# Moving a per-head normalisation and its bias tile from VectorE to GpSimd, in the differential attention of a two-block transformer kernel

## What is computed

```python
s  = einsum(q, k) * 64**-0.5 + slope[head] * (k_pos - q_pos)     # for both maps, masked to k <= q
a  = softmax(s[map 0]) - lam * softmax(s[map 1])
o  = a @ v                                                       # 512 x 128 for one head
o  = rms_norm(o, out_g) * (1 - lam_init)                         # over the 128 channels of the head
y  = o * silu(az)
```

## Time and profile before

| | us |
|---|---|
| median of 3 runs (2393.18 to 2393.83) | 2393.45 |
| the profiled execution | 2402.3 |
| its span | 2400.5 |
| TensorE busy | 2286.0 (95%) |
| VectorE busy | 1370.9 (57%) |
| ScalarE busy | 1004.8 (42%) |
| GpSimd busy | 262.2 (11%) |
| granted TensorE clock, mean | 0.972 |

### The profile page before, as it was taken

The page is one execution under the profiler, slowest core; times in us unless marked ns, Lnnn a source line. Parts: engine busy times, 40 slices in busy tenths (PEclk is TensorE's granted clock), DMA queues, the critical chain, the costliest instruction groups (busy, mean ns, idle before and its releaser), DMA issues. The chain is left out here.

```text
span 2400.5 us, 30388 instructions
## 1 busy us (share of the span) xinstructions
PE 2286.0 (95%) x11223; PEld 1849.9 (77%) x11223; DVE 1370.9 (57%) x2905; ACT 1004.8 (42%) x1896; POOL 262.2 (11%) x350
## 2 busy tenths in 40 slices
PE   5899989899999999999889999999999989999999
PEld 4777767688777787778778888888878657888887
DVE  6956676756746454554563455445455595545543
ACT  5545645433454545453323333233434583322322
POOL 3641000016101011100000000000011240000000
PEclk9999999899999999999877999999999999999999
DMA  7354112134332222225474232232322102233222
GB/s 207 119 163 140 54 53 88 36 106 141 106 102 71 84 92 84 75 75 184 134 200 109 76 104 86 92 105 88 105 88 88 53 2 71 88 105 106 80 88 96
DMA packets 192800, 236.73 MB, mean 99 GB/s; under 512 B 38827, under 2 KB 120194, under 8 KB 192654
## 3 DMA queue, kind: packets, MB, share of 16 engines
q1 hardware_dynamic: 170910, 211.93, 27.8%
q10 hardware_dynamic: 21744, 22.84, 3.0%
HBM read 215.84 MB, written 23.09 MB: 100 GB/s over the span
## 5 line engine op out<-in xcount | busy, mean ns | idle before, releaser
L2125 PE MATMUL G<-w_hi,u_hi 128*128 128x512 f32 x1536 | 624.3, 406 | 10.8 <-issue 5.6
L1666 DVE SCALAR_TENSOR_TENSOR w_lo<-raw,par,w_hi 128x512 fp32r<-128x512 f32 x496 | 368.1, 782 | 433.9 <-ACT w_hi L1134 431.0
L2127 PE MATMUL G<-w_hi,u_lo 128*128 128x512 f32 x1536 | 602.6, 392 | 0.0
L2126 PE MATMUL G<-w_lo,u_hi 128*128 128x512 f32 x1536 | 601.9, 392 | 0.0
L1134 ACT ACTIVATE w_hi<-raw,par 128x512 fp32r<-128x512 f32 x496 | 317.5, 715 | 378.4 <-PE G L2127 365.0
L2125 PE MATMUL G<-u_hi,w_hi 128*128 128x512 f32 (+1 forms) x1168 | 462.1, 396 | 11.8 <-DVE u_lo L1732 11.8
L2126 PE MATMUL G<-u_lo,w_hi 128*128 128x512 f32 (+1 forms) x1168 | 450.1, 385 | 0.0
L2127 PE MATMUL G<-u_hi,w_lo 128*128 128x512 f32 (+1 forms) x1168 | 450.0, 385 | 0.0
L2125 PEld LDWEIGHTS G<-w_hi,u_hi 128*128 128x128 f32 x1536 | 290.5, 189 | 78.7 <-issue 13.3
L2127 PEld LDWEIGHTS G<-w_hi,u_lo 128*128 128x128 f32 x1536 | 290.4, 189 | 63.2
L2126 PEld LDWEIGHTS G<-w_lo,u_hi 128*128 128x128 f32 x1536 | 290.9, 189 | 60.0 <-issue 1.9
(11 more groups left out here) (304 smaller groups left out, 2389.0 us busy)
## 6 DMA issues: line engine op xcount, KB each, us to landing
raw<-in_ffn_w_up SPq DMA_DIRECT2D x88, 512.0 KB, 4.6
raw<-in_e_w_in SPq DMA_DIRECT2D x56, 512.0 KB, 4.7
raw<-in_o_w_in SPq DMA_DIRECT2D x56, 512.0 KB, 4.5
raw<-in_ffn_w_down SPq DMA_DIRECT2D x40, 512.0 KB, 4.4
raw<-in_e_w_out SPq DMA_DIRECT2D x16, 512.0 KB, 4.6
raw<-in_o_w_out SPq DMA_DIRECT2D x16, 512.0 KB, 4.2
raw<-in_a_w_glu SPq DMA_DIRECT2D x16, 512.0 KB, 4.4
raw<-in_w_kv SPq DMA_DIRECT2D x16, 512.0 KB, 4.3
```

What stands on the lines that cost most here:

```text
L1666: V.scalar_tensor_tensor(w_lo[:, n % HL, k], raw[:, n % RAW, k], gain(name, k0 + k), w_hi[:, n % HL, k].bitcast(F32), ALU.mult, ALU.subtract)\
L2125: pe.matmul(out, lh, rh, start=start, stop=False)
L2126: pe.matmul(out, lh, rl, start=False, stop=False)
L2127: return pe.matmul(out, ll, rh, start=False, stop=stop)
```

## The change

The normalisation of a head's output and the bias of a head go from VectorE to GpSimd. ScalarE sums the squares itself, in four instructions with an accumulator where there was one. GpSimd then issues 17 linked instructions on 128x4 values (VectorE's form had 12, with one shift and three fused ones; here are a conversion through float and plain products) and the 128x512 product. The bias of an odd head lies in `big[:, 18]`, that of an even one in `junk[:, 1]`, and each has a semaphore `bias_ready`. VectorE's product to `y` goes from the end of the BACK slot to its beginning. GpSimd's work for heads 0 and 1 stands at the group's first unit, for heads 2 and 3 five units later, between the squares of two query and key chunks.

```diff
@@ Pool
+            def pool_bias(s, hd):
+                before, t = (s, 4 * hd - 5) if hd > 1 else (s.scored, len(s.scored.steps) - 1)
+                pool.wait_ge(*at_("score", before.i, t))
+                if hd == 1 and before.akind == "X":
+                    pool.wait_ge(*at_("y", before.i, before.heads - 1))
+                pool.tensor_scalar(head_bias(hd), bias_tile[:, :], 2.0 ** -(s.y0 + hd + 1), None, ALU.mult)\
+                    .then_inc(*by("bias_ready", s.i, hd))
+
+            def pool_head_norm(s, hd):
+                tt, ts = pool.tensor_tensor, pool.tensor_scalar
+                on = junk[:, 0, :].rearrange("p (a b) -> p a b", b=P)
+                pool.wait_ge(*at_("o_squared", s.i, hd))
+                do(ts(oss, oss, 1.0 / P, EPS, ALU.mult, ALU.add))
+                do(pool.tensor_copy(oln, oss.bitcast(I32)))
+                do(ts(oln, oln, -0.5, float(0x5f3759df), ALU.mult, ALU.add))
+                do(pool.tensor_copy(orstd.bitcast(I32), oln))
+                do(ts(oss, oss, -0.5, None, ALU.mult))
+                for _ in range(3):
+                    do(tt(oln, orstd, orstd, ALU.mult))
+                    do(tt(oln, oln, oss, ALU.mult))
+                    do(ts(oln, oln, 1.5, None, ALU.add))
+                    do(tt(orstd, orstd, oln, ALU.mult))
+                pool.wait_ge(*at_("o_copied", s.i, hd))
+                tt(on, o_copy.rearrange("p (a b) -> p a b", b=P), orstd.unsqueeze(2).to_broadcast([P, TT, P]), ALU.mult)\
+                    .then_inc(*by("on_ready", s.i, hd))
...
+                for s in a_mix:
+                    if s.n == n:
+                        for hd in range(3):
+                            pool_bias(s, hd)
+                        pool_head_norm(s, 0)
+                        pool_bias(s, 3)
+                        pool_head_norm(s, 1)
+                    if s.n + 5 == n:
+                        pool_head_norm(s, 2)
+                        pool_head_norm(s, 3)
@@ Activation
-                    nc.scalar.activation(junk[:, 0, :], X[:, s.aux["pv", hd] % 4, :], ACT.Square)\
-                        .then_inc(*by("o_squared", s.i, hd))
+                    for i in range(TT):
+                        c = slice(P * i, P * i + P)
+                        ins = nc.scalar.activation(junk[:, 0, c], X[:, s.aux["pv", hd] % 4, c], ACT.Square,
+                                                   accum_out=oss[:, i:i + 1])
+                    ins.then_inc(*by("o_squared", s.i, hd))
@@ DVE, dve_slot
+                if is_last(s, t - BACK) and s.akind == "A":
+                    hd = s.steps[t - BACK][0]
+                    y = big[:, s.y0 + hd, :]
+                    a = s.aux["ot", hd]
+                    dve.wait_ge(*at_("gate", s.gate, hd))
+                    dve.wait_ge(*at_("aux_ready", a))
+                    V.scalar_tensor_tensor(y, X[:, a % 4, :], gain("aout"), y, ALU.mult, ALU.mult)\
+                        .then_inc(*by("y", s.i, hd))
                 if t < T:
...
                     if s.akind == "A" and i == 0:
-                        link("dve", dve, V.tensor_scalar(junk[:, 1, :], bias_tile[:, :], 2.0 ** -(head + 1), None,
-                                                         ALU.mult))
+                        dve.wait_ge(*at_("bias_ready", s.i, hd))
...
-                    if s.akind == "A":
-                        on = junk[:, 0, :].rearrange("p (a b) -> p a b", b=P)
-                        dve.wait_ge(*at_("o_squared", s.i, hd))
-                        link("dve", dve, V.tensor_reduce(oss, on, AX_X, ALU.add))
-                        inverse_rms(orstd, oss, P, oln)
-                        dve.wait_ge(*at_("o_copied", s.i, hd))
-                        V.tensor_tensor(on, o_copy.rearrange("p (a b) -> p a b", b=P),
-                                        orstd.unsqueeze(2).to_broadcast([P, TT, P]), ALU.mult)\
-                            .then_inc(*by("on_ready", s.i, hd))
...
-                if is_last(s, t - BACK) and s.akind == "A":
-                    hd = s.steps[t - BACK][0]
-                    y = big[:, s.y0 + hd, :]
-                    a = s.aux["ot", hd]
-                    dve.wait_ge(*at_("gate", s.gate, hd))
-                    dve.wait_ge(*at_("aux_ready", a))
-                    V.scalar_tensor_tensor(y, X[:, a % 4, :], gain("aout"), y, ALU.mult, ALU.mult)\
-                        .then_inc(*by("y", s.i, hd))
```

More of the change, by code:

```diff
@@ L420, in attention @@
             s.n = state["n"]
+            if kind == "A":
+                a_mix.append(s)
+                for hd in range(heads):
+                    mark("bias_ready", s.i, hd)
             s.steps = [(hd, TT - 1 - i if kind == "C" else i) for hd in range(heads) for i in range(TT)]
@@ L528, in plan_ffn @@
             plan_down(22).first_y = first_y
+        a_mix = []
         def plan_even():
@@ L548, in plan_even @@
                              ("v", "N", dict(dst=8))], hosts)
+                scored = before
                 before, at = attention("A", 4, 4 * g, len(plan)), 7
-                if g == 0:
-                    a_mix = before
+                before.scored = scored
                 plan_chunks([("silu", "T", dict(dst=4 * g))], [(before, -1)])
@@ L555, in plan_even @@
             state["e_down"] = plan_down(16)
-            state["e_down"].first_y = ("y", a_mix.i, 3)
+            state["e_down"].first_y = ("y", a_mix[0].i, 3)
         c_mix = []
@@ L807, in scores, with head_bias @@
             return (att[:, 16 + m, :], att[:, 18 + m, :], third)[t % 3]
+        def head_bias(hd):
+            return big[:, 18, :] if hd % 2 else junk[:, 1, :]
         def sb_keep(t):
@@ L1811, in dve_slot @@
                             if s.akind == "A":
-                                b = junk[:, 1, 384 - P * i:512]
+                                b = head_bias(hd)[:, 384 - P * i:512]
                             else:
@@ L1837, in dve_slot @@
                             .then_inc(*by("p_ready", s.i, t - 1))
-                if is_last(s, t - VALUE):
+                if is_last(s, t - VALUE) and s.akind != "A":
                     hd = s.steps[t - VALUE][0]
                     y = big[:, s.y0 + hd, :]
-                    if s.akind == "A":
-                        on = junk[:, 0, :].rearrange("p (a b) -> p a b", b=P)
-                        dve.wait_ge(*at_("o_squared", s.i, hd))
-                        link("dve", dve, V.tensor_reduce(oss, on, AX_X, ALU.add))
-                        inverse_rms(orstd, oss, P, oln)
-                        dve.wait_ge(*at_("o_copied", s.i, hd))
-                        V.tensor_tensor(on, o_copy.rearrange("p (a b) -> p a b", b=P),
-                                        orstd.unsqueeze(2).to_broadcast([P, TT, P]), ALU.mult)\
-                            .then_inc(*by("on_ready", s.i, hd))
-                    else:
-                        a = s.aux["pv", hd]
-                        dve.wait_ge(*at_("gate", s.gate, hd))
-                        dve.wait_ge(*at_("aux_ready", a))
-                        V.tensor_tensor(y, X[:, a % 4, :], y, ALU.mult).then_inc(*by("y", s.i, hd))
-                if is_last(s, t - BACK) and s.akind == "A":
-                    hd = s.steps[t - BACK][0]
-                    y = big[:, s.y0 + hd, :]
-                    a = s.aux["ot", hd]
+                    a = s.aux["pv", hd]
                     dve.wait_ge(*at_("gate", s.gate, hd))
                     dve.wait_ge(*at_("aux_ready", a))
-                    V.scalar_tensor_tensor(y, X[:, a % 4, :], gain("aout"), y, ALU.mult, ALU.mult)\
-                        .then_inc(*by("y", s.i, hd))
+                    V.tensor_tensor(y, X[:, a % 4, :], y, ALU.mult).then_inc(*by("y", s.i, hd))
             def dve_prep(s, t):
```

## The result

The changed kernel takes 2402.79 us (median of 6 runs, 2399.14 to 2407.49), the kernel before 2394.91 us in the runs beside it: ratio 1.0031, 95% interval 1.0018 to 1.0045, which is 4 to 11 us more. One of the six executions of the kernel before took 3770.46 us and is not in the ratio; the median of the other five is 2393.83 us. The sign is as forecast, the size is not: 27 us were forecast. The profiled execution is 2403.86 us with a span of 2402.1 us. The profiled execution of before lay above its own median, so the two spans can't be subtracted from each other; the stage can be compared by its events.

A forecast was written before the change was run, and what follows sets the result against it. TensorE, busy 95%, was taken as the bound, so only its waits count: +34 new waits, -18.7 old waits, +20 clock lost, -8.7 clock regained is +27 us, 2420 us, stated as 2419; range 2384 to 2452.

The forecast's parts named there:

- The bound and the waits removed: TensorE's waits in the differential attention: 18.7 us in all, of which 9.3 us for y and 5.8 us for scores go.
- The new wait: TensorE in the BACK slot waits for GpSimd's normalised output: chain 10.4 us against 6.1 us, 4.3 us per head, 34 us.
- Squares to the first small instruction: ScalarE's four squares with accumulators, 1.6 us, and 0.1 us to hand over: 1.7 us per head.
- Small instructions: 17 linked ones on GpSimd at 0.27 us, 4.6 us per head, plus 2.8 us of disturbance by VectorE.
- Product and hand-over: GpSimd's 128x512 product, 1.06 us, 1.1 us with its hand-over, per head.
- The clock: Each of eight 4.3 us waits lowers TensorE's clock: 20 us lost, against 8.7 us gained from waits removed.
- Of my rivals the first: Same GpSimd wait, but the clock falls no more than now: +16 us, 2409 us; chance 0.15.
- rival 2: GpSimd's chain runs undisturbed, 7.6 us; TensorE waits 1.5 us per head; net -12 us, 2381 us; chance 0.17.
- Rivals 3 and 4: 3: chain disturbed all through, +70 us, 2463 us, chance 0.10; 4: waits only change names, 2393 us, chance 0.06.
- GpSimd's other work: Squares per chunk shift by some us, hidden; three early biases, about 0.6 us each, are made slots ahead.

The follow-up runs named there:

- e1: Kernel before with VectorE's y of a finished head put first in its slot, nothing moved to GpSimd; ratio to before 0.9962.
- e4: Changed kernel with the BACK slot one later (7 for 6), so TensorE asks for the normalised output later; ratio to before 0.9907.
- e8: Changed kernel with nine more linked 128x4 instructions in GpSimd's chain of each head; ratio to before 1.0150.
- e12: Changed kernel with VectorE filling w_lo with zeros in units 18 to 31 instead of computing it; ratio to before 0.9988.
- e3: Changed kernel with the normalisation back on VectorE and one square instruction on ScalarE; biases stay on GpSimd, y first; ratio to before 0.9957.
- e5: Kernel before with only the BACK slot one later; ratio to before 0.9978.

## Why the prediction was wrong, point by point

**The bound and the waits removed: right.** The 18.7 us of waits were the right account. e1 shows that y first takes 8 of the 9.3 us of y waits; with the normalisation off VectorE the score waits are gone in the changed kernel.

**The new wait: right mechanism, a failed size, 34 us forecast, 23.5 us measured.** TensorE's slack from the squares' start came out at 6.0 us (forecast 6.1 us). The chain was 8.9 us where I had 10.4 us. By terms:
- Squares to the first small instruction: 1.2 us for 1.7 us. A 128x128 square with its accumulator repeats every 0.25 us; I had taken the exponential's 0.40 us.
- Small instructions: 6.6 us on average for 4.6 + 2.8 us. Undisturbed ones repeat every 0.28 us (0.27 us forecast), 4.8 us for 17; the disturbance is 1.8 us, not 2.8 us. I counted all of VectorE's time with these instructions in 8 us after the squares as delay, but the small instructions run for 6.6 us only, and one that is held lasts as long as VectorE's beside it, with its own 0.28 us inside that time. In head 0 VectorE's weights and w_lo pieces run for 3.3 us beside the chain and delay it by 2.2 us.
- Product and hand-over: 1.1 us, as forecast; the further 0.2 us for hand-overs was counted twice.

So 1.5 us per head too much, 11 to 12 us for eight.

One reading was wrong beside it: of the two instructions that make a step's weights, the scaling (L1832, L1890 in the changed kernel) reads one SBUF tile, not two. That it belongs among the disturbers all the same is seen in e4, at the end.

**The clock: the other step that failed, as large as the first.** "Waits of 4.3 us should each bring it", 20 us less the 8.7 us gained. It was worked out for a wait I had over-sized, and the eight as if equal. They run from 1.7 to 4.6 us, and four of them brought no fall of the clock. The other four brought 3.4, 1.7, 3.4 and 1.7 us of missing clock time, 10.2 us in all, as much as before, so in the traces this term of +11 us is 0. The runs agree: of the 4 to 11 us measured, 6.3 us are waits, which leaves -2 to +5 us for the clock. e8 shows that the rule was fit for the waits it assumed: with eight waits of 4.4 to 7.3 us 27.3 us are missing, of which 18 us lie outside the waits, where the rule has 20 us. Two smaller readings were off as well: of the clock time missing before, 0.6 us falls into idle time and not 1.7 us, and the fall behind the wait of 2.60 us cost 3.4 us and not 2.9 us.

**Together:** 23.5 + 1.5 of waits, less 18.7, and no change of clock is +6.3 us, inside the measured 4 to 11 us. The forecast was +27 us: too high by 11 us for the over-sized chain (34 for 23.5) and by 11 us for the clock, too low by 1.5 us for waits that stayed. Of my rivals the first, with the clock as now, had the right account and the wrong chain.

**The other side** (rival 2, undisturbed chain) failed for the reason given: w_lo and the weights fall into those microseconds, and e12 measures one of the two. e4 gets below its 2381 us, but not in its way: the small instructions take 6.7 us there, as long as in the changed kernel, and TensorE asks later.

**Rivals 3 and 4.** The chain was not disturbed all through: in head 0 five of 17 small instructions took 0.58 to 0.68 us, one 0.32 us and the rest 0.19 to 0.23 us. And the waits did not only change their names: their sum went from 18.7 to 25.0 us, and e1 alone takes 6 us away.

**GpSimd's other work** was hidden as said; the biases took 1.5 us each where I said 0.6 us, at no cost that e3 could show.

## What to carry to other kernels

Before moving a serial chain to an idle engine, measure the slack of its consumer from the event that starts the chain, and lay every link of the chain against it: here 6.0 us against 8.9 us, and 0.34 to 0.41 us of wait for each small instruction on GpSimd. The idle engine stops costing time once the consumer is put a slot later (1.0031 to 0.9907), so move the consumer with the producer. Then test whether the idle engine is needed at all: with the chain left on VectorE and only the sums and the bias moved, the kernel is at 0.9926 without the later slot and at 0.9921 with it. A change in the waits counts a second time through the clock, but not in proportion: work the clock out wait by wait, not for the mean wait.

## What the runs showed of the hardware

- GpSimd's multiplication of a 128x512 fp32 tile by a constant took 1.49 to 1.83 us in the changed kernel, longer than its product of two tiles, 1.04 us.
- The disturbance goes both ways. In e4 GpSimd's product (first row) holds up VectorE's scaling of the weights (second row), which takes 0.49 us elsewhere. The product starts 0.15 us earlier, and the scaling ends 0.28 us after it:

```profile
436.29 1.04 POOL L1092 TENSOR_TENSOR work<-big,small 128x512 f32<-128x512 f32 x1
```

```profile
436.44 1.17 DVE L1890 TENSOR_SCALAR big<-big,small 128x512 f32<-128x512 f32 x1
```

  The Trainium skill (SBUF — State Buffer, section Who interferes with whom) says that such a VectorE instruction can take a mode that uses the shared port pair, and that whoever comes first keeps it. The rows agree. That mode is the exception to the rule for VectorE instructions with one SBUF input, and the prediction gave the rule without it.
- Not every wait brought the granted clock down to half. In this stage, in the traces of all 14 kernels, every wait of 3.0 us or more did. Of the twelve waits of 2.6 to 2.8 us seven did and five did not: 2.60 us in the kernel before did, 2.61 us in the changed kernel (head 2 above) did not. In e5 one wait of 1.01 us did and another of the same length did not. What decides between these is open.
- A stretch at half clock lasted about 3.5 us or about 7 us in these traces (1.7 or 3.4 us of missing clock time), two of each in the changed kernel.
